# The up product of a gated feed-forward block by seven block products in place of eight

## The reference

```
g, v = split(x @ w_up, 2)            # w_up: 1024 x 5632, g and v 2816 wide each
g = g[t-1]*cw[0] + g[t]*cw[1] + g[t+1]*cw[2] + cb     # within each sequence
ffn = (gelu(g) * v) @ w_down         # w_down: 2816 x 1024
gate = sigmoid(x @ w_ple_gate + b_ple_gate)
x = layer_norm(ALPHA*x + ffn + gate * (p @ w_ple))
```

## Time and profile before

| | us |
|---|---|
| median of three runs | 1203.26 |
| the profiled execution, span from first to last instruction | 1201.6 |
| the profiled execution's end-to-end time | not listed |
| PE busy | 1187.7 |
| POOL, DVE, ACT busy | 585.3, 522.3, 483.7 |

### The profile page before, as it was taken

The page is one execution under the profiler, slowest core; times in us unless marked ns, Lnnn a source line. Parts: engine busy times, 40 slices in busy tenths (PEclk is TensorE's granted clock), DMA queues, the critical chain, the costliest instruction groups (busy, mean ns, idle before and its releaser), DMA issues.

```text
span 1201.6 us, 16482 instructions
## 1 busy us (share of the span) xinstructions
PE 1187.7 (99%) x5784; PEld 972.2 (81%) x5784; DVE 522.3 (43%) x1094; ACT 483.7 (40%) x890; POOL 585.3 (49%) x338
## 2 busy tenths in 40 slices
PE   8999999999999999999999999999999999999997
PEld 6887778888888888888888777788888888888886
DVE  7777857522122134211587787474221122441107
ACT  3456763344334333323144767433443333332310
POOL 6665854465444444344264756634644444434330
PEclk9999999999999999999999999999999999999999
DMA  6321222344323332223132202433433333223311
GB/s 224 87 78 46 89 59 100 127 135 124 105 87 89 103 106 90 86 93 104 53 88 71 81 26 71 140 105 88 140 109 101 103 89 99 94 75 101 105 35 70
DMA packets 121754, 113.45 MB, mean 94 GB/s; under 512 B 6753, under 2 KB 97889, under 8 KB 121697
## 3 DMA queue, kind: packets, MB, share of 16 engines
q1 hardware_dynamic: 121696, 112.71, 30.3%
HBM read 110.60 MB, written 2.10 MB: 94 GB/s over the span
## 4 chain that ended last, share of the span: by engine, by line
PE 97%; DVE 1%; POOL 1%; DMA 1%; DVEq 1%; issue 0%; SPq 0%
PE ps L1240 29%; PE ps L1241 29%; PE ps L1242 29%; PE ps L1406 3%; PE ps L1392 3%; PE ps L1380 1%; PE ps L1382 1%; PE ps L1250 1%; PE ps L1363 1%; DMA x<-in_x_prompt_dram 1%; POOL w_lo L545 1%; DVEq L887 0%; POOL ln_r L541 0%; PE ps L1417 0%; DVE bn L1222 0%; PE ps L1462 0%
## 5 line engine op out<-in xcount | busy, mean ns | idle before, releaser
L535 POOL TENSOR_TENSOR w_lo<-raw,w_hi 128x1024 fp32r<-128x1024 f32 x188 | 453.1, 2412 | 404.7 <-ACT w_hi L646 404.5
L1240 PE MATMUL ps<-xt_hi,w_hi 128*128 128x512 f32 x704 | 273.9, 389 | 0.0
L1241 PE MATMUL ps<-xt_lo,w_hi 128*128 128x512 f32 x704 | 273.9, 389 | 0.0
L1242 PE MATMUL ps<-xt_hi,w_lo 128*128 128x512 f32 x704 | 273.9, 389 | 0.0
L646 ACT ACTIVATE w_hi<-raw 128x1024 fp32r<-128x1024 f32 x188 | 197.8, 1055 | 132.6 <-PE ps L1242 63.0
L1240 PE MATMUL ps<-w_hi,stat 128*128 128x512 f32 x480 | 187.8, 391 | 0.0
L1241 PE MATMUL ps<-w_lo,stat 128*128 128x512 f32 x480 | 187.1, 390 | 0.0
L1242 PE MATMUL ps<-w_hi,stat 128*128 128x512 f32 x480 | 187.0, 390 | 0.0
L1240 PEld LDWEIGHTS ps<-xt_hi,w_hi 128*128 128x128 f32 x704 | 132.1, 188 | 27.7
L1242 PEld LDWEIGHTS ps<-xt_hi,w_lo 128*128 128x128 f32 x704 | 132.1, 188 | 27.4
L1241 PEld LDWEIGHTS ps<-xt_lo,w_hi 128*128 128x128 f32 x704 | 132.1, 188 | 27.2
(11 more groups left out here) (123 smaller groups left out, 1322.2 us busy)
## 6 DMA issues: line engine op xcount, KB each, us to landing
raw<-in_w_up_dram SPq DMA_DIRECT2D x88, 512.0 KB, 3.8
raw<-in_w_down_dram SPq DMA_DIRECT2D x44, 512.0 KB, 3.2
raw<-in_w_in_dram SPq DMA_DIRECT2D x22, 512.0 KB, 3.8
raw<-in_w_out_dram SPq DMA_DIRECT2D x16, 512.0 KB, 3.3
raw<-in_w_ple_gate_dram SPq DMA_DIRECT2D x16, 512.0 KB, 3.3
scratch<-in_ln_g_dram SPq DMA_DIRECT2D x5, 512.0 KB, 4.5
scratch<-in_ln_b_dram SPq DMA_DIRECT2D x5, 512.0 KB, 6.2
raw<-in_w_ple_dram SPq DMA_DIRECT2D x4, 512.0 KB, 3.3
```

Source lines behind the costliest of these rows:

```text
L535: pool.tensor_tensor(w_lo[:, n, :], raw[:, n % RAW, :], w_hi[:, n, :].bitcast(F32), ALU.subtract).then_inc(w_split.sem, 1)
L1240: pe.matmul(out, a[0], b[0], start=first, stop=False)
L1241: pe.matmul(out, a[0], b[1], start=False, stop=False)
L1242: return pe.matmul(out, a[1], b[0], start=False, stop=last)
```

## The change

The up product of a tile is a 2 x 2 block product: the weights' blocks are (upper or lower 512 rows) x (g or v), the blocks of x the same row halves x (first or second sequence). In place of eight block products it makes seven, p1 to p7, of sums of blocks (Strassen's scheme in Winograd's form). Each is 4 row blocks x 3 matmuls of 256 columns.

- Four sums of x (t1 to t4) are made once a layer in the gate stage: ACT keeps an unsplit copy of the transposed x (`x_raw`), DVE adds (`t_add`), ACT and DVE split (`t_high`, `t_low`).
- For each tile m the pair of pieces goes to `raw` (odd m) or to free parts of `stat` (even m). POOL makes two differences in one instruction (`up_corners` less block 2) into `sums`, DVE the two inner sums (`pair_sums`) into PSUM banks 4 and 5. ACT makes four high parts (`outer_hi`, `corner_hi`, `inner_hi`, `pure_hi`), POOL three low parts, DVE one (`inner_low`).
- Products share banks and accumulate; ACT takes three snapshots a tile (`snap`, `snap_product`), and DVE adds them back (`v_sum`, `g_sum`).
- Three pairs of banks in turn; all loops of the up and down product are written out. All h tiles keep a buffer until the down product splits them (`h_at`). The loads of the second norm's constants move into the down product.

The core of the diff (the buffers' views, the renaming of slots and the signals' declarations are left out):

```diff
+UP_BANKS = ((2, 3), (6, 7), (0, 1))
+REST_ORDER = (0, 4, 5, 1, 2, 3)
+def up_phases():
+    order = []
+    for j in range(FT):
+        order += [("p1", j), ("p2", j), ("p5", j), ("p6", j)]
+        if j == FT - 1:
+            order += [("p3", j - 1), ("p7", j), ("p4", j - 1)]
+        else:
+            if j:
+                order += [("p3", j - 1), ("p4", j - 1)]
+            order.append(("p7", j))
+    order += [("p3", FT - 1), ("p4", FT - 1)]
+    a, b = order.index(("p7", 0)), order.index(("p1", 1))
+    order.insert(a, order.pop(b))
+    return order
...
 # SP
+                sp.wait_ge(w_used.sem, w_used.at(layer, GATE_AT))
+                for m in range(FT):
+                    if m == 1:
+                        sp.wait_ge(w_split.sem, w_split.at(layer, UP_AT - AHEAD))
+                    if m >= 2:
+                        sp.wait_ge(pair_inner.sem, pair_inner.at(layer, m - 1))
+                        sp.wait_ge(pair_lo.sem, pair_lo.at(layer, 3 * (m - 1)))
+                    for value in range(2):
+                        dst = raw[:, value, :] if m % 2 else stat_f[:, value, 0:2, :].rearrange("p a n -> p (a n)")
...
+                sp.wait_ge(pair_inner.sem, pair_inner.at(layer, FT))
+                sp.wait_ge(pair_lo.sem, pair_lo.at(layer, 3 * FT))
+                for n in range(LOOPED + 1):
+                    if n >= RAW:
+                        raw_free(DOWN_AT + n)
+                    load(DOWN_AT + n, down_source(layer, n - 1 if n else LOOPED), 1)
...
 # POOL
+                for m in range(FT):
+                    outer, corner, pure = (up_place(layer, m, n) for n in (0, 1, 3))
+                    pool.wait_ge(pair_landed[m % 2].sem, pair_landed[m % 2].at(layer, 32 * (m // 2 + 1)))
+                    if m:
+                        pool.wait_ge(pair_inner.sem, pair_inner.at(layer, m))
+                        pool.wait_ge(pair_lo.sem, pair_lo.at(layer, 3 * m - 1))
...
+                    pool.tensor_tensor(scratch[:, 0:2, :], up_corners(m), up_block(m, 2).unsqueeze(1).to_broadcast([P, 2, 512]),
+                                       ALU.subtract).then_inc(pair_outer.sem, 1)
+                    pool.wait_ge(pair_hi.sem, pair_hi.at(layer, 4 * m + 1))
+                    pool.tensor_tensor(w_lo[:, outer, :], up_outer_rows(m), w_hi[:, outer, :].bitcast(F32),
+                                       ALU.subtract).then_inc(pair_lo.sem, 1)
+                    pool.wait_ge(pair_hi.sem, pair_hi.at(layer, 4 * m + 2))
+                    pool.tensor_tensor(w_lo[:, corner, :], sums, w_hi[:, corner, :].bitcast(F32),
+                                       ALU.subtract).then_inc(pair_lo.sem, 1)
+                    pool.wait_ge(pair_hi.sem, pair_hi.at(layer, 4 * m + 4))
+                    pool.tensor_tensor(w_lo[:, pure, 0:512], up_block(m, 3), w_hi[:, pure, 0:512].bitcast(F32),
+                                       ALU.subtract).then_inc(pair_lo.sem, 1)
...
 # ACT
                 gate(0, 1)
+                t_high(1)
                 body_hi(29)
                 gate(0, 2)
+                t_high(2)
                 gate(0, 3)
+                t_high(3)
+                outer_hi(0)
                 gate(1, 0)
+                corner_hi(0)
+                inner_hi(0)
+                pure_hi(0)
                 gate(1, 1)
                 gate(1, 2)
                 gate(1, 3)
+                for j in range(FT + 1):
+                    if j >= 2:
+                        gelu(j - 2)
+                    if j == 0:
+                        outer_hi(1)
+                        snap(0, 0)
+                        t_high(4)
+                    elif j < FT:
+                        snap(j, 0)
+                    if 0 < j < FT - 1:
+                        outer_hi(j + 1)
                     if j < FT - 1:
+                        corner_hi(j + 1)
+                    if j == FT - 1:
+                        body_hi(DOWN_AT)
+                        act.wait_ge(pair_lo.sem, pair_lo.at(layer, 3 * (FT - 1)))
+                        rest_hi(0)
+                    if j < FT:
+                        snap_product(j)
+                        snap(j, 1)
                     if j < FT - 1:
+                        inner_hi(j + 1)
+                    if j == FT - 1:
+                        body_hi(DOWN_AT + 1)
+                    if j == FT:
+                        looped_h(0)
+                    if j:
+                        conv_centre(j - 1)
+                    if j < FT - 1:
+                        pure_hi(j + 1)
+                    if j == FT - 1:
+                        body_hi(DOWN_AT + 2)
+                        body_hi(DOWN_AT + 3)
+                gelu(FT - 1)
+                body_hi(DOWN_AT + 4)
+                body_hi(DOWN_AT + 5)
+                for v in range(LOOPED):
+                    if v:
+                        looped_h(v)
+                    if v < REST - 1:
+                        rest_hi(REST_ORDER[v + 1])
+                    body_hi(DOWN_AT + 6 + v)
...
 # DVE, after gate_apply of q
+                    if q == 0:
+                        t_add(1)
+                    if q == 1:
+                        t_low(1)
+                        t_add(2)
+                    if q == 2:
+                        t_add(3)
+                        t_low(2)
+                    if q == 3:
+                        t_add(4)
+                        t_low(3)
+                    if q == 4:
+                        pair_sums(0)
+                    if q == 5:
+                        inner_low(0)
+                for j in range(FT + 1):
+                    if j:
+                        v_sum(j - 1)
+                    if j >= 2:
+                        glu(j - 2)
+                    if j == 0:
+                        t_low(4)
+                    if j < FT - 1:
+                        pair_sums(j + 1)
+                    if j == FT - 1:
+                        rest_low(0)
+                    if j == FT:
+                        looped_low(0)
+                    if j:
+                        g_sum(j - 1)
+                    if j < FT - 1:
+                        inner_low(j + 1)
+                    if j:
+                        conv_sides(j - 1)
+                glu(FT - 1)
...
+                def pair_sums(m):
+                    dve.wait_ge(pair_outer.sem, pair_outer.at(layer, m + 1))
+                    dve.drain()
+                    dve.tensor_tensor(ps[:, 4, :], scratch[:, 1, :], up_block(m, 0), ALU.add)
+                    dve.drain()
+                    dve.tensor_tensor(ps[:, 5, :], up_block(m, 1), ps[:, 4, :], ALU.subtract).then_inc(pair_inner.sem, 1)
...
 # PE
+                for name, j in PHASES:
+                    if name == "p1":
+                        pe.wait_ge(pair_lo.sem, pair_lo.at(layer, 3 * j + 1))
+                        if j == 0:
+                            pe.wait_ge(t_split.sem, t_split.at(layer, 3))
+                        elif j == 1:
+                            pe.wait_ge(gate_in.sem, gate_in.at(layer, 8))
+                        elif j == 2:
+                            pe.wait_ge(t_split.sem, t_split.at(layer, 4))
+                        else:
+                            pe.wait_ge(h_done.sem, h_done.at(layer, j - 2))
+                    elif name == "p5":
+                        pe.wait_ge(pair_lo.sem, pair_lo.at(layer, 3 * j + 2))
+                    elif name == "p6":
+                        pe.wait_ge(inner_split.sem, inner_split.at(layer, j + 1))
+                        pe.wait_ge(snapped.sem, snapped.at(layer, 3 * j + 1))
+                    elif name == "p7":
+                        pe.wait_ge(snapped.sem, snapped.at(layer, 3 * j + 3))
+                    elif name == "p3":
+                        pe.wait_ge(snapped.sem, snapped.at(layer, 3 * j + 2))
+                    elif name == "p4":
+                        pe.wait_ge(pair_lo.sem, pair_lo.at(layer, 3 * j + 3))
+                        pe.wait_ge(v_summed.sem, v_summed.at(layer, j + 1))
...
+                    up_product(name, j)
```

More of the change, by code:

```diff
@@ L58 @@
 UP_AT = 30
-DOWN_AT = UP_AT + 2 * FT
+DOWN_AT = UP_AT
 STREAM = DOWN_AT + FT
@@ L469, in _ @@
                     load(s, source(s, layer), 2)
[L471 to L477, removed]
@@ L641, in _, with norm_hi @@
         def _(act):
[L642 to L648, removed]
+            def norm_hi(t, full, keep=False):
                 for b in range(2):
@@ new lines, in v_sum, with g_sum @@
+                def v_sum(j):
+                    v = UP_BANKS[j % 3][1]
+                    wait_phase(dve, layer, "p7", j)
+                    dve.wait_ge(snapped.sem, snapped.at(layer, 3 * j + 2))
+                    dve.tensor_tensor(ps[:, v, SEQ:TOK], ps[:, v, 0:SEQ], snap_five(layer, j), ALU.add).then_inc(v_summed.sem, 1)
+                def g_sum(j):
+                    g = ps[:, UP_BANKS[j % 3][0], :]
+                    wait_phase(dve, layer, "p3", j)
```

(24 more changed lines are left out.)

359 lines of the change are left out of this document (233 added, 126 removed).

## The result

The changed kernel takes 1213.45 us (median of 4 runs, 1210.64 to 1215.55) beside 1203.22 us for the kernel before: ratio 1.0083, 95% interval 1.0067 to 1.0099. It is slower by 0.8%, 10 us, where 6.5 us less was forecast. The profiled execution took 1212.13 us, 1210.3 of it span; before it was 1201.6, so 8.7 us of the difference can be looked for in the two traces.

A forecast was written before the change was run, and what follows sets the result against it. PE's matmul start-to-start distance was taken as the bound. Two layers: 38.9 us saved by PE less 32.4 of waiting gave -6.5, so 1203.3 becomes 1196.8 us; range 1168 to 1222.

The forecast's parts named there:

- stop in the gate stage: Gate stage, per layer: added DVE work delays gate sums and PE loses 2.8 us, bounds 0 and 11.3.
- stops at the start of up: Start of the up product, per layer: late snap, outer_lo(1) and a table load cost PE 4.3 us, bounds 0 and 7.
- stops at the end of up, in down: End of up into down, per layer: late down weights and full queues cost PE 9.1 us, bounds 0 and 12.
- The fourth token tile's 4.9: First down tile: PE waits for glu(21)'s bank from 17.8 to 22.7 us after the last up tile's start, 4.9 lost.
- The second looped tile's 3.3: Down product: body_hi(36), waiting for its load, stands ahead of looped_h(1) on ACT; PE loses 3.3 us.
- The rest of the down product gets its tiles faster (6.8 us for two) than PE uses them: Later down product: two tiles supplied in 6.8 us, PE uses 5.44 each.
- 16.2 of waiting against 19.45 saved: Whole sum per layer: waits of 2.8, 4.3 and 9.1 us set against PE's saving; -6.5 us over two layers.
- I take 119, the row of the same shape: Up product's 256-column matmuls start 119 ns apart, between bounds of 113 and 188; PE loses 38.9 us in two layers.
- rival C: Up product: weight load not quite hidden in long runs; gain gone from 120.8 ns, 1219 us at 125 ns; chance 0.14.
- Rival D: Up product: each pass waits for its own 188 ns weight load, 1419 us; chance 0.01.
- Rival B: Up product loop: the POOL-DVE chain becomes the bound, 10.4 to 10.5 us a tile, 1217 us; chance 0.20.
- Rival A: Stage borders: queue orders leave slack, all waits are hidden and PE's full saving stays, 1164.4 us; chance 0.18.

The follow-up runs named there:

- the second experiment: Changed kernel with ScalarE making the high parts of the third and fourth down pieces after the last gelu: 1213.35 us, ratio 1.0087.
- the first experiment: Changed kernel with SyncE issuing the second norm's constant loads behind the loop over the 17 down pieces: 1203.76 us, ratio 1.0003.
- The last experiment: Changed kernel with the up product's matmuls made on 192 of their 256 columns, other columns left out: one run, 1202.1 us.

## Why the prediction was wrong, step by step

Stops of PE in the profiled execution, layer 0 / layer 1, against the terms of the sum (us):

| term | predicted | measured |
|---|---|---|
| matmuls of the up product | -19.45 | -17.2 / -17.2 |
| stop in the gate stage | 2.8 | 2.2 / 2.0 |
| stops at the start of up | 4.3 | 3.2 / 3.2 |
| stops at the end of up, in down | 9.1 | 11.4 / 10.8 |
| matmuls at half speed | none | 3.0 / 5.7 |

- **The sum of the stops was right by luck, with one cause missing and others too dear.** 16.8 and 16.0 against 16.2 a layer. The gate stage's 2.2 stands whole at the fourth gate tile, where 1.4 was forecast. The fourth token tile's 4.9 came out at 4.8 at the place and for the reason given, as the second experiment shows. The second looped tile's 3.3 came out at 2.0 and 0.8. The sentence "The rest of the down product gets its tiles faster (6.8 us for two) than PE uses them" failed: it left out that the change put the norm loads, and the wait ahead of them, into SP's queue between the down pieces. That is 3.2 and 3.0 us at the looped tile 3, and 9.6 us of the time as the first experiment has it, with what follows from it.
- **The step that turned the sign: "16.2 of waiting against 19.45 saved" priced a stop at its idle time only.** PE comes back from most of the long stops at half speed: 42 matmuls, 8.7 us in two layers. Without these the sum with the measured terms would still be a gain of 1.6. Nothing in the forecast's sum, and no rival, had them, though the trace of before shows such matmuls near the program's start, behind PE's one long stop. Its timeline there:

```profile
18.89 0.40 PE L1242 MATMUL ps<-w_hi,xt_lo 128*128 128x512 f32 x1
21.43 0.50 PE L1240 MATMUL ps<-w_hi,xt_hi 128*128 128x512 f32 x1 [2.14 <-POOL w_lo L545]
...
22.56 0.63 PE L1240 MATMUL ps<-w_hi,xt_hi 128*128 128x512 f32 x1
22.98 0.63 PE L1241 MATMUL ps<-w_lo,xt_hi 128*128 128x512 f32 x1
```

  A stop of 2.3 us there had seven matmuls at half speed behind it, 1.3 us (granted clock 0.52 from 21.7 to 24.8); stops of 2.5, 4.9 and 3.3 us were forecast in each layer.
- **"I take 119, the row of the same shape" was 1 ns short.** In the long run the spacing is 120.2: (226.45 - 4.2 of stops) / 1848. That is 2.2 us a layer, 4.4 in all. It is rival C in direction, below its break-even of 120.8. The last experiment shows why the lower bound of 113, half of 226.7, was out of reach: at 192 columns the spacing is still 111. Rival D's 188 is out.
- **The loop was charged rightly with nothing.** Its chain is 9.64, predicted 9.9, against PE's 10.08. Rival B is out. The block sums on GpSimd took the 2.4 chosen; one low part of 1024 took 2.85 in place of 2.4 (L747), for which no run shows the reason, so GpSimd works 9.0 of a tile's 10.08 us and not 8.4. DVE's add had to wait the GpSimd instruction out. Groups of DVE's two sums and GpSimd's block sums in the up product of layer 0:

```profile
L1386 DVE TENSOR_TENSOR ps<-scratch,stat_f 128x512 f32<-128x512 f32 x10 | 28.2, 2820 | 9.9 <-POOL scratch L741 9.9
L1388 DVE TENSOR_TENSOR ps<-raw,ps 128x512 f32<-128x512 f32 x11 | 7.7, 697 | 0.8
L741 POOL TENSOR_TENSOR scratch<-stat_f 128x1024 f32<-128x1024 f32 x10 | 24.2, 2421 | 0.0
```

  The Trainium skill's page SBUF — State Buffer, section SBUF: two separate sides, has this as an exclusive lock for the whole instruction; 2820 ns for the add of two SBUF operands beside 697 for the one with a PSUM operand agrees.
- **The sum with the measured terms**: -34.4 + 32.8 + 8.7 = +7.1. The stages differ by 8.4, the spans by 8.7 and the medians by 10.2; the 1.3 between the first two are not placed.
- **Rival A** (all stops hidden, 1164.4) was a matter of order, not of work: the same instructions, three queues (SP, ACT, DVE) reordered, give 1179.7. What still lies above it is the 4.4 of spacing, some 4 us of stops a layer at the start and the end of the up product, and matmuls at half speed behind the longest stop of either layer (2.4 and 2.1 us; granted clock 0.50 from 253.9 to 257.0 and from 830.5 to 833.9).

## What to carry to other kernels

When a stage that feeds PE is rebuilt, walk every in-order queue across both of its borders, SP's too, and look behind each instruction that waits for a DMA: whatever PE needs next must stand ahead of it, or the stop only moves from tile to tile until the whole order is right. Price a stop of PE with the half-speed matmuls that the trace shows behind other stops. A forecast that is the small difference of two sums of some 35 us has no sign until each term is known within a few us.

## What was not expected of the hardware

- Behind stops of 2.0 to 4.8 us, 6 to 12 matmuls ran at half the clock (0.427 for 0.227 us); with cheap matmuls in the 4.8 us stop none did. A stop of 3.2 us in layer 0 was followed by full speed, one of 3.0 in layer 1 by eight slow matmuls.
- Float32r matmuls with a full weight load each: 227 ns at 512 columns, 120 at 256, 111 at 192.
